# Another order of steps for TensorE and its helpers in the mixer of a hybrid decoder layer, and two table loads moved behind a spill on the DMA queue

## The reference

```
proj = rmsnorm(x) @ w_in                               # q, k, v, a, b, z, and B, C, h of the short convolution
q, k, v = split(silu(conv4(proj_qkv)));  q, k l2-normalised
log_a, beta from proj_a, proj_b;  g = cumsum(log_a) within a chunk
A = I + strict(beta * (k k^T) * exp(g_i - g_j))        # per chunk and head
u, w = A^-1 [v beta | k beta exp(g)]                   # triangular solve
for each chunk:  v_new = u - w S;  o = q exp(g) S + (q k^T decay) v_new
                 S = S exp(g_last) + (k exp(g_last - g))^T v_new
o = rmsnorm(o) * silu(z);  y_sc = B * conv3(C * h)
x = x + [o, y_sc] @ w_out;  then MLP, per-layer embedding, final norm
```

## Time and profile before

| | us |
|---|---|
| median of 3 runs | 1527.79 |
| lowest, highest | 1526.78, 1531.0 |
| the profiled run | 1531.0 |
| its span | 1529.0 |
| TensorE busy | 1488.9 |
| VectorE busy | 722.4 |

### The profile page before, as it was taken

One profiled execution on the slowest core, in us unless ns is written; L12 is line 12 of the kernel. 1 busy time (PEld: TensorE's weight loads), 2 busy tenths in 40 slices (PEclk: granted clock), 3 DMA queues, 4 the chain that ended last, 5 costly groups with the idle time before them and its releaser, 6 DMA issues.

```text
span 1529.0 us, 24976 instructions
## 1 busy us (share of the span) xinstructions
PE 1488.9 (97%) x9412; PEld 1453.4 (95%) x9412; DVE 722.4 (47%) x1305; ACT 483.5 (32%) x878; POOL 249.5 (16%) x306
## 2 busy tenths in 40 slices
PE   7999899999999999999999999999999999998997
PEld 6999898899999899899999999999999999998997
DVE  5676943568674622543333334333333334335525
ACT  5313343323424432533122131221303122135525
POOL 3200312054443722100000000000000000040303
PEclk9999998999999999999999999999999999999998
DMA  7112312303123233111111111111111111112002
GB/s 175 45 39 56 93 35 63 122 29 84 57 56 105 60 90 93 33 42 55 42 42 55 42 41 49 48 42 42 55 42 42 56 42 42 55 42 70 29 29 114
DMA packets 140203, 89.82 MB, mean 59 GB/s; under 512 B 16203, under 2 KB 134155, under 8 KB 140118
## 3 DMA queue, kind: packets, MB, share of 16 engines
q1 hardware_dynamic: 139110, 84.89, 19.2%
q0 software_dynamic: 1008, 3.79, 0.6%
HBM read 77.97 MB, written 10.69 MB: 58 GB/s over the span
## 4 chain that ended last, share of the span: by engine, by line
PE 90%; DVE 4%; issue 1%; POOL 1%; ACT 1%; DMA 0%; DVEq 0%; POOLq 0%; ACTq 0%; SPq 0%
PE pg L696 66%; PE pg L814 13%; PE bk L871 1%; DVE act_lo L2002 1%; PE bk L889 1%; PE bk L885 1%; PE bk L1042 1%; POOL act_lo L2311 1%; PE bk L1022 1%; PE bk L841 0%; PE bk L931 0%; PE bk L934 0%; PE bk L902 0%; PE bk L922 0%; PE bk L939 0%
## 5 line engine op out<-in xcount | busy, mean ns | idle before, releaser
L696 PE MATMUL pg<-act_hi,w_hi 128*128 128x352 f32 x1344 | 438.3, 326 | 12.5 <-issue 4.6
L696 PE MATMUL pg<-act_lo,w_hi 128*128 128x352 f32 x1344 | 432.4, 322 | 0.0
L696 PE MATMUL pg<-act_hi,w_lo 128*128 128x352 f32 x1320 | 423.3, 321 | 0.0
L696 PEld LDWEIGHTS pg<-act_hi,w_hi 128*128 128x128 f32 x1344 | 253.2, 188 | 16.4 <-issue 8.9
L696 PEld LDWEIGHTS pg<-act_lo,w_hi 128*128 128x128 f32 x1344 | 253.9, 189 | 0.0
L696 PE MATMUL pg<-u_hi,w_hi 128*128 128x352 f32 x768 | 249.3, 325 | 0.0
L696 PE MATMUL pg<-u_hi,w_lo 128*128 128x352 f32 x768 | 248.9, 324 | 0.0
L696 PE MATMUL pg<-u_lo,w_hi 128*128 128x352 f32 x768 | 247.8, 323 | 0.0
L696 PEld LDWEIGHTS pg<-act_hi,w_lo 128*128 128x128 f32 x1320 | 247.5, 188 | 0.0
L1165 ACT ACTIVATE w_hi<-w_raw 128x1024 fp32r<-128x1024 f32 x111 | 116.9, 1053 | 366.9 <-PE pg L696 304.0
L2352 POOL TENSOR_TENSOR ssq<-ssq,sq 128x352 f32<-128x352 f32 x72 | 78.1, 1099 | 892.4 <-ACT sq L1165 891.5
(11 more groups left out here) (333 smaller groups left out, 1663.9 us busy)
## 6 DMA issues: line engine op xcount, KB each, us to landing
w_raw<-in_w_up SPq DMA_DIRECT2D x32, 512.0 KB, 4.0
w_raw<-in_w_down SPq DMA_DIRECT2D x32, 512.0 KB, 3.3
w_raw<-in_w_in SPq DMA_DIRECT2D x29, 512.0 KB, 4.0
x_tok<-in_x_prompt SPq DMA_DIRECT2D x8, 512.0 KB, 7.4
w_raw<-in_w_out SPq DMA_DIRECT2D x8, 512.0 KB, 5.0
x_col<-in_x_prompt SPq DMA_DIRECT2D x8, 512.0 KB, 3.6
w_raw<-in_w_ple_gate SPq DMA_DIRECT2D x8, 512.0 KB, 3.9
out<-y_tok SPq DMA_DIRECT2D x8, 512.0 KB, 2.7
```

The costliest lines, as they stand in the source:

```text
L696: last = mm(pg[bank][:, 0:TH], w, a, start=i == 0, stop=i == len(terms) - 1)
```

## The change

The table has the same 188 steps and the same 1440 fills, but other numbers of fills behind the steps and, from `vturn 0` on, another order of the steps. The first steps (`begin` to `s_put 7`) keep their order; only the fills between them change. A line of the table before and after:

```
-s_solve 0 0 19; s_out 0 0 4; s_onorm 0 0 11; s_put 0 0 5; s_put 1 0 6; s_put 2 0 11; s_put 3 0 0; s_put 4 0 4;
+s_solve 0 0 34; s_out 0 0 5; s_onorm 0 0 13; s_put 0 0 1; s_put 1 0 0; s_put 2 0 4; s_put 3 0 0; s_put 4 0 1;
```

The code of SP changes in one place:

```diff
                 elif k == "vturn" and c == 0:
                     for h in range(H):
                         sp.wait_ge(sm.s_out_made, 2 * (h + 1))
-                        if h == H - 1:
-                            sp.wait_ge(sm.q_o, 1)
-                            load_rows(2)
-                            load_rows(3)
                         sp.dma_start(os_s[0, :, h, :, :].rearrange("b d e -> d b e"), S_in[:, h, :, :]) \
                             .then_inc(sm.sample_states_out, 16)
                     for x in range(2):
                         sp.wait_ge(z_spilled[x], 16 * (NSC // 2))
                     sp.dma_start(qkv[:, H:2 * H, TP:T], z_dram[:, :, TP:T].rearrange("h p t -> p h t")) \
                         .then_inc(sm.zs_loaded, 16)
+                    sp.wait_ge(sm.q_o, 1)
+                    load_rows(2)
+                    load_rows(3)
```

More of the change, by code:

```diff
@@ L60 @@
[L60 to L74, removed]
@@ L75 @@
-tail 0 0 0
+begin 0 0 51; diff 0 0 3; diff 1 0 6; kk 0 0 27; kk 1 0 0; kq 0 0 6; b1 0 0 2; b2 0 0 15; b3 0 0 0; b4 0 0 0;
+kq 1 0 29; turned 0 0 5; turned 1 0 45; y 0 4 0; y 1 4 21; z 0 4 4; z 1 4 18; y 0 5 0; y 1 5 18; z 0 5 37;
+z 1 5 1; y 0 6 33; y 1 6 0; z 0 6 24; z 1 6 14; s_wait 0 0 0; s_begin 0 0 17; s_norm 0 0 0; s_conv 0 0 28;
+s_kk 0 0 12; s_conv 1 0 15; s_xt 0 0 0; s_conv 2 0 0; s_y 0 0 6; s_z 0 0 0; s_state 0 0 15; s_turn 0 0 6;
+s_solve 0 0 34; s_out 0 0 5; s_onorm 0 0 13; s_put 0 0 1; s_put 1 0 0; s_put 2 0 4; s_put 3 0 0; s_put 4 0 1;
@@ new lines @@
+s_put 5 0 6; s_put 6 0 0; s_put 7 0 42; vturn 0 0 33; diff 2 0 1; diff 3 0 0; vturn 1 0 0; kk 2 0 0; kq 2 0 0;
+kturn 0 0 13; into 0 0 8; kk 3 0 10; solve 0 0 0; b1 2 0 0; b2 2 0 8; b3 2 0 6; b4 2 0 0; kq 3 0 13;
+turned 2 0 1; update 0 0 12; sum 0 0 22; turned 3 0 21; y 2 4 12; y 3 4 0; z 2 4 2; into 1 0 0; norm 0 0 3;
+z 3 4 3; kturn 1 0 29; y 2 5 4; y 3 5 0; z 2 5 4; solve 1 0 0; z 3 5 2; update 1 0 5; y 2 6 0; sum 1 0 0;
+y 3 6 9; scale 0 0 0; z 2 6 7; norm 1 0 8; z 3 6 4; scale 1 0 9; vturn 2 0 2; diff 4 0 9; vturn 3 0 5;
@@ new lines @@
+diff 5 0 0; kk 4 0 18; kk 5 0 3; into 2 0 1; b1 4 0 0; b2 4 0 0; kq 4 0 0; b3 4 0 3; b4 4 0 0; kturn 2 0 32;
+solve 2 0 5; turned 4 0 13; kq 5 0 22; turned 5 0 6; update 2 0 0; y 4 4 1; sum 2 0 7; y 5 4 0; z 4 4 0;
+into 3 0 4; norm 2 0 10; kturn 3 0 0; z 5 4 9; y 4 5 4; solve 3 0 0; y 5 5 0; z 4 5 10; update 3 0 0; z 5 5 12;
+sum 3 0 12; y 4 6 0; y 5 6 2; norm 3 0 0; scale 2 0 0; z 4 6 0; z 5 6 0; scale 3 0 11; vturn 4 0 0;
+vturn 5 0 1; diff 6 0 0; diff 7 0 16; kk 6 0 3; kk 7 0 0; into 4 0 5; b1 6 0 6; kturn 4 0 18; b2 6 0 0;
@@ new lines @@
+kq 6 0 23; solve 4 0 27; kq 7 0 0; b3 6 0 4; b4 6 0 0; turned 6 0 13; turned 7 0 0; update 4 0 10; sum 4 0 23;
+y 6 4 0; y 7 4 0; z 6 4 0; into 5 0 0; norm 4 0 0; z 7 4 19; y 6 5 0; kturn 5 0 6; solve 5 0 0; y 7 5 5;
+z 6 5 13; z 7 5 0; update 5 0 0; sum 5 0 11; scale 4 0 0; y 6 6 4; y 7 6 8; z 6 6 4; norm 5 0 0; z 7 6 0;
+scale 5 0 4; vturn 6 0 6; vturn 7 0 7; into 6 0 0; kturn 6 0 17; solve 6 0 11; update 6 0 0; sum 6 0 9;
+kturn 7 0 15; into 7 0 5; norm 6 0 20; solve 7 0 11; update 7 0 0; sum 7 0 22; scale 6 0 28; norm 7 0 0;
@@ L76 @@
+scale 7 0 4; tail 0 0 0
 """
```

## The result

The changed kernel takes 1544.51 us (median of 4 runs, 1543.38 to 1545.03); the kernel before, run beside it, 1527.28 us (4 runs, 1525.52 to 1531.0). The ratio is 1.0108 with a 95% interval of 1.0089 to 1.0129, so it is slower by 14 to 20 us, 17.2 by the medians. The profiled executions differ by less, 1544.85 against 1531.0, since that of before was the slowest of its four runs. Their spans are 1542.9 and 1529.0: +13.9.

The account below looks back on a forecast made before the run. TensorE's work and waits were taken as the bound. The terms 1.7 + 4.1 + 1.7 + 3.4 + 3.0 = 13.9 on the profiled 1531.0 gave 1544.9, against the median 1541.7, stated as 1541 us; range 1530 to 1549.

Parts of the forecast that it names:

- The bound: Whole kernel: TensorE's work plus its waits sets the time; the change can only alter its waits or low clock time.
- Early steps, +1.7: Chunks 0 and 1: VectorE idles 1.1 us more and `PT` of `kq 1` adds 0.6, so the second wait ends later.
- Gate rows, +4.1: At `kk 3`: late rows delay both `diff`s and ScalarE's copies; a 5.6 us wait comes, 1.50 at `kk 2` goes.
- The clock behind that wait, +1.7: Behind the wait of `kk 3`: one low clock stretch of 3.4 us, costing half its length, 1.7 us.
- State steps, +3.4: `s_y`, `s_z`, `s_state` in one block: 17 us at low clock, 8.5 lost against 5.1 before.
- `s_put`, +3.0: Eight `s_put`s with 12 fills: 14 us at low clock, 7 lost against 3.4 before; +3.0 taken.
- The rest, 0: From fill 712 to the table's end: no added wait counted, at most +2 us.
- From the profile to the median, -3.2: Whole kernel: the profiled run before lies 3.2 us above its median, so 1544.9 becomes 1541.7.
- only the waits count: Whole kernel: low clock stays the same in sum, +7.5 us, 1535; chance 0.25 shared with the rows in time.
- the rows of gates come in time: At `kk 3`: spill and read overlap more, no wait, +6.6 us, 1534; chance 0.25 shared with only waits counting.
- no measurable change: Samples' steps: narrow blocks cost one low stretch each, so +2.4 us in all, 1530; chance 0.12.
- Faster by the clock alone: Early and samples' steps: all seven low stretches go, -6.1 us, 1522; chance 0.08 with anything else faster.

Follow-up runs that it names:

- both pairs: Old against new fills behind the first 13 steps, compared in the changed kernel (old put back: 1542.64 us) and in the kernel before (new put in: 1526.42 us).
- the new fills: The changed kernel's fills behind the first 13 steps; put alone into the kernel before: 1526.42 us, ratio to before 1.0010.
- the old fills: The kernel before's fills behind the first 13 steps; put back alone into the changed kernel: 1542.64 us, ratio to before 1.0106.
- Taking away cause and wait together: Changed kernel with only the two gate row loads back ahead of the fourth state output: 1535.59 us, ratio to before 1.0055.
- the three places undone: Changed kernel with gate rows ahead again and the fills among the `s_put`s and among `s_y` to `s_turn` as before: 1527.59 us, ratio 1.0017.
- spaced: Changed kernel with the old fills put back among the `s_put`s (1536.67 us) or, separately, behind `s_y` to `s_turn` (1540.39 us).
- woven kernel: Changed kernel, the three places undone, plus one fill behind each sequence's 8 columns in the state steps and evenly spaced `s_put`s: 1523.24 us, ratio 1.0003.
- the other: The woven kernel with the kernel before's fills behind the first 13 steps: 1522.77 us, ratio to before 0.9985.

## Why the prediction was right, and where its sizes were off

The forecast was 1541 us, 1530 to 1549, slower at 0.80. The time is 1544.5: the sign, the range and the place of each cost are right, and the sum for the profiled run (+13.9, 1544.9) is what the profiled run took (1544.85). That closeness is partly luck: the early steps were 1.5 us too large, the clock behind `kk 3` 1.2 and the `s_put`s 1.5 too small, and 1.3 us fell away at the program's start, which no term had.

- **The bound.** That only TensorE's waits and its clock could change the time held. The matmuls are the same in number, 7.5 us of the 13.9 are busy time at low clock, the rest waits.
- **Early steps, +1.7: VectorE's part right, the sum wrong.** The idle of 1.9 (measured 1.97), the `PT` ahead of the evacuation, the wait of 6.3 (6.2) and the end 1.7 later (1.7 in both pairs) all came. The step that failed is the silent one, that the low stretch behind the second wait stays. That it might go was named beside the lower bound (whose -1.7 is more than one stretch can give: 1.7 - 1.7 is 0), and is what happened in all eight profiles with the new fills: net +0.2 in the profile. The medians give 0.9 one way and 1.9 (0.3 by the ratios) the other, and one profile with the old fills was 1.8 us shorter than this kernel's: the cost in a usual run is open between 0 and 2 us. The second wait is 0.9 to 2.4 us in the eight profiles instead of 3.1, and no low stretch followed it.
- **Gate rows, +4.1: right** (5.84 - 1.50 = +4.3). F, the end of fill 575, is 289.9 now. The read is issued at F + 7.1 (predicted 7.1), the rows at F + 7.5 (7.5), VectorE is done at F + 13.8 (13.4), ScalarE's copies at F + 15.5 (15.2), TensorE arrives at F + 9.8 (9.6). The wait is 5.84 (5.6). VectorE's 0.4 us more are the rows, which took 4.1 to 4.4 us to land and not 3.6 to 4.0 as in the earlier trace rows. The fixed cost of about 2 us in the Trainium skill, "DMA: Bandwidth & Descriptors", section "Anatomy of one DMA — SWDGE (gpsimd) path", would alone have made the wait 3.8; it is given there for DMAs that GpSimd issues, with a term for the size on top, and these loads of 256 KB are issued by SP. With 4.1 to 4.4 us the trace does not bear it out as their whole cost.
- **The clock behind that wait, +1.7: mis-sized.** It was low for 6.8 us, not 3.4, and TensorE was at work for 5.85 of them: +2.9. Taking away cause and wait together gave 8.9 (8.1 by the ratios; 8.9 from fill 592 to 1439 in the profiles), and 5.8 + 2.9 = 8.7 were to go.
- **State steps, +3.4: right** in mechanism and size. 17 us low were forecast, 17.1 came; the part cost +3.7, with 0.8 us of a new wait for ScalarE's copy in it that was counted as nothing. The exact 17.1 is luck: four other kernels with this order had 13.7. The difference to the order of before was much the same there (35.4 against 31.5 and 31.8).
- **`s_put`, +3.0: right, 1.5 too small.** 14 us low were forecast, 17.1 came, +4.5. The 0.6 us taken off for the four and six fills in between was wrong, as they didn't shorten the low time; the larger part is that the clock stayed low through some 6 us of fills behind the last `s_put`.
- **The rest, 0: right.** Behind fill 712 the changed order has one wait of 0.6 us in the table. With the three places undone, all that is left of the change, early steps included, costs about 2 us (ratio 1.0005 to 1.0030), which leaves the rest within the +2 given for it.
- **From the profile to the median, -3.2: wrong.** The sum was made against a profiled run 3.2 above its median, and this was carried over. The changed kernel's profiled run is only 0.3 above its own. The median difference is 17.2, and the 3.3 us between it and 13.9 are nearly the whole miss of the forecast (3.5). Part of it can be read: the profile of before was low for 6.8 us at the program's start, that of changed for 3.4 (1.3 us by fill 0), where eight of the twelve profiles have 6.8 and four 3.4; and from fill 500 to 592 the old order of the `s_put`s took 27.4 us in the profile of before, but 24.3 and 25.9 in those of the two kernels that have it unchanged, while the changed order took 31.9 in all five. (The state steps were slow in both profiles, 33.3 for 31.5 and 31.8, and 37.0 for 35.4, so they don't enter.) The profile that the sum rested on, with a granted clock of 0.987, held more low clock than a usual run of that kernel (0.989 in the median of 63).

Of the rivals, "only the waits count" (1535) fell with the 17.1 us stretches, "the rows of gates come in time" (1534) with VectorE's 9.02 us for the DMA, and "no measurable change" with both. "Faster by the clock alone" had one true part, the low stretch behind the second early wait did vanish; of the other six none did. The reason given for taking the middle of the bounds, that a block goes on after its first low stretch with the same work that brought it, agrees with the spaced and woven kernels for the narrow part of the stretches; it does not cover the wide fills at their end. The rule of the Trainium skill, "TensorE: Matmul & The Clock Gate", section "What's actually happening", is that the low clock is the default and activity releases it. It says nothing of narrow work, and taken as busy time it does not fit this trace: TensorE's records have no gap in those 17.1 us, and it stayed at 1.2 GHz.

What stays open: why the same spacing of the `s_put`s had 6.8 us of low clock in one kernel and none in another, why the late rows cost 8 to 9 us in one order and 3 in the other, and what puts 3 of 11 runs of the woven kernel, and 1 of 12 of the other, some 10 us above the rest. It is the clock in these too: it was 0.985 and 0.983 over these runs, against 0.989 to 0.994 in the others, and the difference of 0.007 over 1523 us of a busy TensorE is an estimated 11 us. Where in the program it fell isn't known; only one execution of each has a trace.

## What to carry to other kernels

Follow a moved load to the last engine that waits for it, by the queue that issues it: two loads put behind a wait for another engine's spill cost 8 to 9 us in one order of the steps and 3 in another, and moving one of the two engines out from behind them gave back at most 2. When TensorE is the bound, blocks of narrow matmuls can be dear twice, by themselves and by the clock. Here one wide matmul behind each sequence's narrow ones took the low clock of the state steps away; the same wide matmuls in a lump behind the block did not. And a difference of some microseconds is taken from medians; the profile that explains it may have been a slow run, so compare the low stretches of several profiles before a correction is carried from one to another.
